# Expert products of a mixture-of-experts step: gate/up by halves of the contraction, one product that folds and turns, input copy on VectorE

## The reference, cut to what matters

```
gates = ...                       # (tokens, 16): two experts per token, the others 0
hid = silu(einsum("nd,edf->nef", xt, w_gate)) * einsum("nd,edf->nef", xt, w_up)   # d = 1024, f = 256
out = einsum("nef,efd->nd", hid * gates[..., None], w_down)
```

## Time and profile before

| | us |
|---|---|
| median of 3 runs (lowest, highest) | 1426.47 (1416.93, 1430.9) |
| profiled execution, its own time | 1415.01 |
| span of the profiled execution, first to last instruction | 1413.2 |
| TensorE busy | 1210.6 |
| VectorE busy | 707.4 |
| ScalarE busy | 434.8 |
| GpSimd busy | 314.7 |

### The profile page before, as it was taken

How to read it: one execution, slowest core, us unless ns; L and a number is a source line. 1 busy time by engine, 2 the same in 40 slices (tenths; PEclk the granted TensorE clock), 3 DMA queues, 4 the chain that set the end, 5 groups by cost and what they waited for, 6 DMA issues and landing times.

```text
span 1413.2 us, 31486 instructions
## 1 busy us (share of the span) xinstructions
PE 1210.6 (86%) x12303; PEld 742.2 (53%) x12303; DVE 707.4 (50%) x1736; ACT 434.8 (31%) x1010; POOL 314.7 (22%) x321
## 2 busy tenths in 40 slices
PE   4899998999999777777787999999899977788980
PEld 1455553555447545544465556556644655555550
DVE  1366886556277222222225777876626732233335
ACT  2100214345342222222223012155643322233332
POOL 3000012312000433433330000114100043444441
PEclk9999999999999999889999999999999999999995
DMA  9866024575606584568485000130060637678715
GB/s 360 265 273 175 12 113 179 180 239 181 238 35 212 166 287 137 163 227 276 147 266 148 0 4 5 49 120 1 1 238 30 206 111 234 217 280 281 272 43 230
DMA packets 139283, 233.23 MB, mean 165 GB/s; under 512 B 24474, under 2 KB 107940, under 8 KB 133040
## 3 DMA queue, kind: packets, MB, share of 16 engines
q1 hardware_dynamic: 120928, 185.13, 39.2%
q0 software_dynamic: 11520, 24.03, 5.0%
q10 hardware_dynamic: 6736, 22.63, 4.1%
HBM read 214.60 MB, written 21.33 MB: 167 GB/s over the span
## 4 chain that ended last, share of the span: by engine, by line
PE 66%; another core or an unknown queue 10%; DVE 8%; issue 6%; DMA 4%; ACT 4%; ACTq 0%; POOL 0%; SPq 0%; POOLq 0%; DVEq 0%
PE ps L1413 23%; PE ps L1751 12%; PE ps L1680 10%; PE ps L1577 4%; DMA region_h<-in_w_ada 3%; PE ps L1439 3%; PE ps L1601 3%; PE ps L1764 3%; PE ps L1592 2%; PE ps L1742 2%; DVE x L928 1%; PE ps L1772 1%; ACT region_proj L880 1%; DVE region_h L928 1%
## 5 line engine op out<-in xcount | busy, mean ns | idle before, releaser
L1035 DVE SCALAR_TENSOR_TENSOR region_bc<-region_conv,vecs,region_bc 128x655 f32<-128x655 f32 x240 | 202.0, 904 | 0.9
L928 DVE TENSOR_TENSOR region_proj<-ps,region_proj 64x128 f32<-64x128 f32 (+1 forms) x103 | 30.4, 295 | 296.5 <-ACT region_proj L889 265.9
L658 POOL DMA_INDIRECT y_rows<-region_proj,row_out x100 | 102.0, 1020 | 267.4 <-DVE token_col L1394 266.5
L1751 PE MATMUL ps<-region_oq,region_conv 128*32 128x128 f32 x3264 | 122.7, 296 | 23.2 <-issue 21.7
L1413 PE MATMUL ps<-region_h,region_weights 128*128 128x128 f32 (+1 forms) x512 | 139.7, 434 | 1.5 <-ACT region_h L713 1.5
L1751 PE MATMUL ps<-region_weights,region_conv 128*32 128x128 f32 x2944 | 110.2, 289 | 25.4 <-issue 19.9
L889 ACT ACTIVATE region_proj<-ps 64x128 f32<-64x128 f32 x100 | 27.4, 274 | 333.4 <-PE ps L1751 185.5
L1751 PEld LDWEIGHTS ps<-region_oq,region_conv 128*32 128x32 f32 x3264 | 100.2, 119 | 37.3 <-issue 32.8
L1413 PEld LDWEIGHTS ps<-region_h,region_weights 128*128 128x128 f32 x512 | 77.6, 191 | 65.5 <-issue 63.7
L642 POOL DMA_INDIRECT region_conv<-h_rows,token_col x100 | 104.0, 1040 | 32.5 <-issue 32.5
L1751 PEld LDWEIGHTS ps<-region_weights,region_conv 128*32 128x32 f32 x2944 | 86.2, 115 | 42.4 <-issue 34.5
(11 more groups left out here) (264 smaller groups left out, 1843.8 us busy)
## 6 DMA issues: line engine op xcount, KB each, us to landing
region_h<-in_w_ada SPq DMA_DIRECT2D x26, 1024.0 KB, 4.9
region_oq<-in_w_ada SPq DMA_DIRECT2D x20, 1024.0 KB, 8.8
region_weights<-in_w_gate SPq DMA_DIRECT2D x16, 1024.0 KB
region_weights<-in_w_up SPq DMA_DIRECT2D x16, 1024.0 KB
region_weights<-in_w_down SPq DMA_DIRECT2D x16, 1024.0 KB
region_oq<-in_w_gate SPq DMA_DIRECT2D x16, 1024.0 KB
region_oq<-in_w_up SPq DMA_DIRECT2D x16, 1024.0 KB
region_oq<-in_w_down SPq DMA_DIRECT2D x16, 1024.0 KB
```

The source lines that it names most:

```text
L658: pool.indirect_dma_start(y_quarters, bass.IndirectOffsetOnAxis(ap=row_out[:, r:r + 1], axis=0), y_sb[r], None).then_inc(y_stored[r], 16)
L928: return nc.vector.tensor_tensor(out, a, b, op)
L1035: ins = nc.vector.scalar_tensor_tensor(acc[:, ct, :], zpad[:, ct, j:j + CONV_OUT], w, acc[:, ct, :], ALU.mult, ALU.add)
L1751: ins = nc.tensor.matmul(ps[U * g:U * g + U, 1, 0:P], xgT[:, k % 2, U * (k // 2):U * (k // 2) + U], wgu[s][:, k, at:at + P], start=(k == 0 ...
```

## The change

Gate/up: instead of eight steps of 128 rows in two column parts per matrix, there are four steps j, and the four column groups hold (half of the contraction, matrix): each group multiplies one block of 128 rows with all 256 columns of the up or the gate matrix. There are 16 matmuls of 256 columns. After them partitions 0 to 63 hold the partial sums of the first half of the contraction (up, gate), and 64 to 127 those of the second half. ScalarE copies all of it, 128x256, to `gu_parts`. Then TensorE multiplies each 128 columns of it with a constant of 64 columns that has a one where p % 64 equals the column (`C_PAIR`): this adds the two halves and turns the tile in one product (`fold_turned`, two matmuls). Silu is taken of the turned gate values, 128x64, by ScalarE, and VectorE multiplies it with the turned up values straight into `hidT`; the copy of the hidden values is gone, and so is its semaphore `hT_copied`.

The copy of the turned input goes from ScalarE to VectorE, as the first instruction of a unit there. Orders after, for unit v:

- TensorE: gate/up of v; turn of the input of v+1; down of v-1 (waits for `hid_ready`); fold and turn of v (waits for `parts_ready`).
- ScalarE: copy of the parts of v (waits for `gu_full`); copy of a gathered input (after a wait for `xT_full`); context part (waits for `row_gain_ready`); Silu of v (waits for `hT_full`); a wait for `hid_ready`.
- VectorE: input copy (waits for `xT_full`); row gain; index column; y of v-1 (waits for `y_full`); product of v (waits for `silu_ready`); token column.
- GpSimd: as before.

TensorE loads the unit count of the next expert after the gate/up products of an expert's first unit, where before it loaded its own count ahead of them.

```diff
--- before.py
+++ after.py
@@ -80,7 +80,8 @@
 C_EMPTY = C_SPARE + NB
 C_EARLIER = C_EMPTY + 1
 C_FOLD = C_EARLIER + PER_GROUP * PER_GROUP
-N_CONST = C_FOLD + EXPERTS
+C_PAIR = C_FOLD + EXPERTS
+N_CONST = C_PAIR + 2 * U
 
 ADA_W = 2048
 ADA_PARTS = 6 * D // ADA_W
@@ -123,7 +124,8 @@
     c[:, C_EMPTY] = NO_ROW + p // U / 4
     m = np.arange(PER_GROUP)
     c[:, C_EARLIER:C_FOLD] = (m[None, :] < m[:, None]).reshape(-1)
-    c[:, C_FOLD:N_CONST] = p[:, None] % 32 == np.arange(EXPERTS)[None, :]
+    c[:, C_FOLD:C_PAIR] = p[:, None] % 32 == np.arange(EXPERTS)[None, :]
+    c[:, C_PAIR:N_CONST] = p[:, None] % (2 * U) == np.arange(2 * U)[None, :]
     return c
 
 
@@ -253,7 +255,8 @@
         proj = PR[:, :].rearrange("p (t n) -> p t n", t=TILES)
         attT = PR[:, 0:4 * TOK].rearrange("p (k t) -> p k t", k=4)
         y_sb = [PR[:, r * QUARTER:(r + 1) * QUARTER] for r in range(RING)]
-        hidT, silu_g, hid = PR[:, 1024:1024 + 2 * U], PR[0:2 * U, 1088:1088 + P], PR[0:2 * U, 1216:1216 + P]
+        hidT, silu_g = (PR[:, a:a + 2 * U].rearrange("p (c n) -> p c n", c=2) for a in (1024, 1088))
+        gu_parts = PR[:, 1152:1152 + QUARTER]
         zpad = CV[:, 0:CC * ZPAD].rearrange("p (k n) -> p k n", k=CC)
         h2s = CV[:, 0:2048].rearrange("p (b n) -> p b n", b=2)
         res_tmp = CV[:, 2048:3072]
@@ -292,6 +295,7 @@
 
         ring_a = Ring([ps[:, b] for b in range(3)], sem("act_bank_full"), sem("act_bank_empty"))
         ada_bank, next_bank = ps[:, 3], ps[:, 7]
+        gu_bank, hid_bank = ps[:, 1, 0:QUARTER], ps[:, 2, 0:P].rearrange("p (c i n) -> p c i n", c=2, i=2)
         unread = ps[:, 3, 0:P]
         ln_bank = ps[:, 6, P:P + ln_half]
         ring_v = Ring([ps[:, b] for b in range(4, 8)], sem("dve_bank_full"), sem("dve_bank_empty"))
@@ -327,7 +331,7 @@
         gathered, tokens_given = [sem(f"gathered{r}") for r in range(RING)], sem("tokens_given")
         xT_full, xT_copied, xg_copied = sem("xT_full"), sem("xT_copied"), sem("xg_copied")
         gu_full, silu_ready, hid_ready = sem("gu_full"), sem("silu_ready"), sem("hid_ready")
-        hT_full, hT_copied = sem("hT_full"), sem("hT_copied")
+        parts_ready, hT_full = sem("parts_ready"), sem("hT_full")
         y_full, y_ready, y_stored = sem("y_full"), sem("y_ready"), [sem(f"y_stored{r}") for r in range(RING)]
         y_loaded, x_final = [sem(f"y_loaded{t}") for t in range(TILES)], sem("x_final")
         ctx_part_ready, row_gain_ready, blocks_ready = sem("ctx_part_ready"), sem("row_gain_ready"), sem("blocks_ready")
@@ -866,11 +870,6 @@
 
                     return 16 * (trips_before + at) + 16 * (l * (2 if r < AHEAD - RING else 1) + 1)
 
-                def copy_turned(n):
-
-                    act.wait_ge(xT_full, n)
-                    nc.scalar.activation(xgT, ps[:, 0, 0:QUARTER].rearrange("p (h n) -> p h n", h=2), ACT.Copy).then_inc(xT_copied, 1)
-
                 def copy_gathered(r, at):
 
                     act.wait_ge(gathered[r], rows_gathered(r, at))
@@ -880,21 +879,25 @@
                     nc.scalar.activation(ctx_part, g2_bc(1), ACT.Copy, scale=slot_ctx[:, bass.ds(w, 1)]).then_inc(ctx_part_ready, 1)
 
                 context_gain(0)
-                copy_turned(units_before + (l + 1))
+                act.wait_ge(xT_full, units_before + (l + 1))
+                nc.scalar.activation(xgT, ps[:, 0, 0:QUARTER].rearrange("p (h n) -> p h n", h=2), ACT.Copy).then_inc(xT_copied, 1)
                 act.sem_inc(xg_copied, 1)
                 copy_gathered(1, 0)
                 with act.Fori(0, trips) as i:
                     for r in range(RING):
-                        act.wait_ge(gu_full, units_before + RING * i + (r + 1))
-                        nc.scalar.activation(silu_g, ps[2 * U:P, 1, 0:P], ACT.Silu).then_inc(silu_ready, 1)
                         done = RING * (trips_before + i) + r
-                        act.wait_ge(xT_copied, done + (l + 1))
-                        copy_turned(units_before + RING * i + (l + r + 2))
-                        act.wait_ge(xg_copied, done + (2 * l + 2))
+                        seen = units_before + RING * i + r
+                        act.wait_ge(gu_full, seen + 1)
+                        nc.scalar.activation(gu_parts, gu_bank, ACT.Copy).then_inc(parts_ready, 1)
+
+                        act.wait_ge(xT_full, seen + (l + 2))
                         copy_gathered((r + 2) % RING, i + (r + 2) // RING)
 
                         act.wait_ge(row_gain_ready, done + 1)
                         context_gain(RING * i + (r + 1))
+
+                        act.wait_ge(hT_full, seen + 1)
+                        nc.scalar.activation(silu_g, hid_bank[:, :, 0, :], ACT.Silu).then_inc(silu_ready, 1)
                         act.wait_ge(hid_ready, done + 1)
 
                 trips_done = act.value_load(blocks[l][0:1, 2 * EXPERTS + 2:2 * EXPERTS + 3], min_val=1, max_val=100)
@@ -1373,8 +1376,8 @@
                         done = RING * (trips_before + i) + r
                         at = RING * i + r
 
-                        dve.wait_ge(silu_ready, done + 1)
-                        tt(hid, ps[0:2 * U, 1, 0:P], silu_g, ALU.mult).then_inc(hid_ready, 1)
+                        dve.wait_ge(xT_full, units_before + at + (l + 2))
+                        nc.vector.tensor_copy(xgT, ps[:, 0, 0:QUARTER].rearrange("p (h n) -> p h n", h=2)).then_inc(xT_copied, 1)
 
                         dve.wait_ge(ctx_part_ready, done + (l + 1))
                         dve.wait_ge(y_ready, done + 1)
@@ -1386,8 +1389,8 @@
                         dve.wait_ge(y_full, units_before + at + 1)
                         nc.vector.scalar_tensor_tensor(y_sb[r], y_bank[:, 0:QUARTER], slot_gates[:, bass.ds(at, 1)], row_gain, ALU.mult, ALU.mult).then_inc(y_ready, 1)
 
-                        dve.wait_ge(hT_full, units_before + at + 1)
-                        nc.vector.tensor_copy(hidT, ps[:, 2, 0:2 * U]).then_inc(hT_copied, 1)
+                        dve.wait_ge(silu_ready, done + 1)
+                        tt(hidT, hid_bank[:, :, 1, :], silu_g, ALU.mult).then_inc(hid_ready, 1)
 
                         s = (r + AHEAD) % RING
                         dve.wait_ge(xg_copied, done + (2 * l + 3))
@@ -1672,7 +1675,7 @@
 
                     bank = ring_a.open(pe, (l, "logits", t))
                     ring_a.wait_empty(pe, (l, "parts", t))
-                    nc.tensor.matmul(bank[:, 0:EXPERTS], parts, con[:, C_FOLD:N_CONST], start=True, stop=True).then_inc(ring_a.full, 1)
+                    nc.tensor.matmul(bank[:, 0:EXPERTS], parts, con[:, C_FOLD:C_PAIR], start=True, stop=True).then_inc(ring_a.full, 1)
 
                 def project(t, j, a, b):
                     bank = ring_v.bank((l, "wo", t, j))
@@ -1745,11 +1748,11 @@
                 def gate_up(s, v):
 
                     pe.wait_ge(xT_copied, v + (l + 1))
-                    for k in range(DK):
+                    for j in range(4):
                         for g in range(4):
-                            at = FF + g * P if g < 2 else (g - 2) * P
-                            ins = nc.tensor.matmul(ps[U * g:U * g + U, 1, 0:P], xgT[:, k % 2, U * (k // 2):U * (k // 2) + U], wgu[s][:, k, at:at + P],
-                                                   start=(k == 0), stop=(k == DK - 1))
+                            half, part = divmod(g, 2)
+                            ins = nc.tensor.matmul(gu_bank[U * g:U * g + U, :], xgT[:, half, U * j:U * j + U], wgu[s][:, 2 * j + half, part * FF:(part + 1) * FF],
+                                                   start=(j == 0), stop=(j == 3))
                     ins.then_inc(gu_full, 1)
 
                 def turn_next(v):
@@ -1761,42 +1764,45 @@
 
                     for h in range(2):
                         for g in range(4):
-                            ins = nc.tensor.matmul(y_bank[U * g:U * g + U, 0:QUARTER], hidT[:, h * U:(h + 1) * U], wdn[s][:, h, g * QUARTER:(g + 1) * QUARTER],
+                            ins = nc.tensor.matmul(y_bank[U * g:U * g + U, 0:QUARTER], hidT[:, h, :], wdn[s][:, h, g * QUARTER:(g + 1) * QUARTER],
                                                    start=(h == 0), stop=(h == 1))
                     ins.then_inc(y_full, 1)
 
-                def turn_hidden(v):
-
-                    pe.wait_ge(hid_ready, v + 1)
-                    pe.sem_inc(pe_passed, 1)
-                    nc.tensor.transpose(ps[:, 2, 0:2 * U], hid, ident[0:2 * U, 0:2 * U]).then_inc(hT_full, 1)
+                def fold_turned(v):
+
+                    pe.wait_ge(parts_ready, v + 1)
+                    for c in range(2):
+                        ins = nc.tensor.matmul(ps[:, 2, 2 * U * c:2 * U * (c + 1)], gu_parts[:, c * P:(c + 1) * P], con[:, C_PAIR:N_CONST], start=True, stop=True)
+                    ins.then_inc(hT_full, 1)
 
                 pe.wait_ge(gathered[0], 16 * (trips_before + (2 * l + 1)))
                 turn(xg[0])
                 first = RING * trips_before
```

(16 more changed lines are left out.)

## The result

The median fell from 1428.68 us (4 runs, 1416.93 to 1450.06) to **1319.05 us** (4 runs, 1316.4 to 1321.22): a ratio of 0.926, 95% interval 0.920 to 0.932. The ratio leaves out the run of 1450.06, 2.3% above the fastest of its kernel, and in the experiments on chip 8 two runs of the kernel before (1453.56 and 1458.49) and one of e8 (1358.62), which were slow in the same way. The forecast was 1350 with a range of 1312 to 1405, and a likeliest case of 1329 to 1369. The direction, the place and the hold behind GpSimd were right; the saving was 97 us where 69 were forecast in the profiled execution (1415.0 to 1318.2), and the experiments will show that the step named as the change's core was not enough to make it.

A forecast was written before the change was run, and what follows sets the result against it. The prediction took a ring through GpSimd's indirect DMAs, which hold TensorE's "done", as the bound. 95 intervals at 4.37 gave 415 against 484.5 us, -69: execution 1415.0 to 1346, median forecast 1350, range 1312 to 1405.

The forecast's parts named there:

- What bounds the kernel: Expert loops: GpSimd's scatter and gather hide TensorE's "done" until about 1.6 us after the gather, a 5.35 us ring.
- A unit is fast when VectorE's eviction waits for nothing but y_full: VectorE in the expert loops: units are slow when Silu stands before the eviction; fast ring 4.43 us, slow 5.35.
- Order on VectorE. This is the change: VectorE's queue: eviction of y, and so the scatter, no longer stands behind Silu; gather to gather 4.37 us.
- rival A: Expert loops: turned input held until after the gather, slow ring stays at 5.23 us a unit; median to 1407; chance 0.17.
- What halves is the number of instructions: Gate/up on TensorE: 64 records become 32; streaming saves nothing, fewer instructions matter where TensorE is held back inside the product.
- The term at nothing: Gate/up's wider passes on TensorE: no streaming time saved; some 0.5 us a unit by the skill would lie beside the ring.
- Rival B: Expert loops: y_full gets out before the gather, TensorE's 3.75 us a unit binds; -128 us, 1290; chance 0.11.
- the term 95 x 4.37 = 415 us: Both layers' expert loops: 95 unit intervals at 4.37 us, against 484.5 us before, saving 69 us.
- Rival C: Expert loops: fold's "done" held until after the next gather, 6.1 us a unit, +95 us, median 1520; chance 0.06.
- Small terms: Costs per unit: gate/up 1.97 us, fold and turn 0.5, input copy 0.417, VectorE net +0.2, ScalarE 0.
- Early count: Block length read one expert ahead: some 21 x 0.65 = 14 us at first units in slow stretches, not counted separately.
- The clock: TensorE's granted clock: 0.92 to 0.93 in slow stretches, not the reason for their pace; first layer near 1 after.

The follow-up runs named there:

- e8: Changed kernel with the copy of the turned input back on ScalarE, behind the copy of the parts; 1341.85 us, ratio 0.947 to the kernel before.
- e4: Kernel before with GpSimd's indirect gather in the expert loops replaced by a plain DMA of fixed rows; 1334.2 us, one run, ratio 0.93.
- e1: Kernel before with VectorE's product of Silu and up values moved behind the eviction of y; 1537.4 us, ratio 1.068.
- e3: Changed kernel with each 256-column gate/up pass split into two of 128, so 64 records; 1418.41 us, ratio 0.984 to the kernel before.
- e5: Kernel before with only gate/up in 256-column passes, 32 records, leaving out part of the values; 1330.86 us, ratio 0.943.
- e2: Kernel before with VectorE's product behind the eviction of y and the input copy first on VectorE; 1530.38 us, ratio 1.063.
- e11: Changed kernel with each expert's unit count loaded ahead of its first unit again; 1287.59 us on chip 7, ratio 0.992 to the kernel before.
- e6: Changed kernel with 128-column gate/up passes and a plain DMA for the gather in the loops; 1319.26 us, one run, ratio 0.93 to the kernel before.
- e7: Changed kernel with a plain DMA of fixed rows for the gather in the loops; 1294.51 us, one run, ratio 0.91 to the kernel before.
- e9: Changed kernel with the down products ahead of the turn of the next input on TensorE; 1276.56 us on chip 7, ratio 0.982 to the kernel before.

## Why the prediction was right, and where it was not

- **What bounds the kernel: right.** The slow units were GpSimd's indirect DMAs holding TensorE's "done". e4 takes away one of them and the unit falls from 5.57 to 4.32. That issue "goes on at full pace beside the scatter" was too broad: the earlier trace rows had it held within a product, 54 of the 97 products of the kernel before are stretched, and e1 has 3.1 us for 1.95.
- **"A unit is fast when VectorE's eviction waits for nothing but y_full": failed as the cause.** "Order on VectorE. This is the change" had this step carry the whole gain. Alone it costs 6.8% (e1); with the copies, the fold and TensorE's order it gains 1.6% and leaves rival A's ring (e3), since the turned input that VectorE now waits for is held as Silu was; the wide passes alone gain 5.7% (e5). Together that is the 7.4%.
- **"What halves is the number of instructions": failed in its price.** It was to matter "where TensorE is held back inside the product", and the sum had nothing for it. It does matter there (54 stretched products before, 7 after), and beyond: 32 records let the signal out at a phase where 64 keep it in, 0.52 against 2.07 us, though not in e8 (1.41).
- **So the number is right in part by luck.** The order that was to take 5.4% off takes 1.6% off without the wide passes, by which the forecast's 1426.5 would have become 1404, at the far end of the range. The term at nothing brought the rest.
- **Rival B was much of the outcome.** "With half the instructions the y_full gets out before the gather" had 0.11. It does so in 34 of 97 units, and a 4.37 and a 3.5 together are two units of TensorE's 3.82 and little more, so TensorE binds in two units of three. That is the whole error of the sum: the term 95 x 4.37 = 415 us was 386.9, 4.07 a unit, 28 us under. The median came 31 under the forecast.
- **Rival C** was to come from a fold whose "done" is late. e1 and e2 come to 6.2 to 6.4, near its 6.1, another way, by a chain through VectorE that the new TensorE order takes apart.
- **Small terms: right, one too low.** Gate/up 1.93 (1.97 forecast; the 0.27 that was added is more than the 0.22 which L1764's 1.07 leaves over four passes of 0.213), input copy 0.42 (0.417), VectorE +0.18 (+0.2), ScalarE 0. The fold takes 0.66, 0.5 was taken; TensorE's own unit is 3.82 where 3.75 was taken.
- **Early count:** 0.65 us at 21 first units was read as the price of the load. With the load back in place (e11, on chip 7) it is 0.13 at most; the late start of the earlier trace rows then was likely the held issue too, which no run shows by itself. It wasn't counted, so no number moved.
- **The clock: right.** 0.99 in both loops, as forecast; e3 has 1.00 and 0.99 and stays at 5.05 and 5.20 us a unit.

The Trainium skill (SBUF — State Buffer, Who interferes with whom) says, of the ports to SBUF, that TensorE never waits on anyone. On chip 7 the traces agree, for issue (every gate/up product of e11 takes 1.93) and signal, 0 of 97 held; on the others they don't, e3 has 93 of 97 held and e1 all 97 stretched. Whether a port has any part in it no run shows. Where the rule holds, the change has its small terms left: e11, the nearest kernel to it there, is at 0.992 of the kernel before.

## What to carry to other kernels

Where a wait on TensorE ends at a fixed distance behind another engine's instruction, change that instruction first (here one edit, e4) and see whether the wait goes: it is the cheapest test of a ring. Price the number of instructions as well as their streaming time, and try every part of a rewrite alone: a part priced at nothing may be the one that pays. And ask on how many chips a gain was seen; a wait that one chip doesn't have is worth nothing there.

## What was not expected of the hardware

- TensorE's completion is seen late while GpSimd runs indirect DMAs: 2.07 us on average for products that end 0.6 to 1.4 us after the scatter's start, with 64 records; with 32 it is 0.52 in the changed kernel, 0.57 in e5 and 1.41 in e8. With a plain gather it is 0.68 and 0.64 with 64 records (e4, e6) and 0.48 with 32 (e7).
- Issue is held as well: a product of 64 records that is still being issued when the gather starts takes 3.1 us in place of 1.95 (e1).
- One chip of the three, 7, doesn't do this. The kernel before runs there in 1293 to 1307 us (19 runs), with medians of 1418.8 to 1439.63 in the other three measurements. Its own trace on that chip was not taken; that the difference is the hold is inferred from the four other kernels. What tells the chips apart stays open.
- The weight loads stand still for 0.41 us ahead of the fold (561.21 in the changed kernel), and so ahead of the turn, where a full stationary tile follows 32-column ones. In e9 fold follows turn and has no such gap, and the unit is 0.14 us shorter. That the change of tile is the reason is inferred. The gap also goes with the passes before it: in the kernel before it is 0.41 behind down's 256 columns and 0.20 behind gate/up's 128 (medians), about two passes each time.
